# Eight small loads of the chunked S5 input issued one per hyena unit over eight units, where there were two per unit over four

## The reference

```python
h_c = modulate(ctx, norm_mix, cshift_mix, cscale_mix)
u_c = h_c @ w_in[:, :1024]                     # S5 input of the context
h_x = modulate(x, norm_mix, shift_mix, scale_mix)
u_x, hy_x, gates_x = split(h_x @ w_in)         # S5 input, hyena (3 x 1024), merge gates (2 x 2048)
y_x = readout(states(u_x, forward, seeded by the context's last state)) \
    + readout(states(u_x, backward, seeded by the context's first state))
x = x + gate_mix * mixer_output(u_x, y_x, hy_x, gates_x)   # GLU, long convolution, merge, w_out
x = x + gate_ffn * swiglu(modulate(x, norm_ffn, shift_ffn, scale_ffn), w_ffn_in, w_ffn_out)
return rms_norm(x, norm_f)
```

## Time and profile before

| | us |
|---|---|
| median of 3 runs | 2881.26 |
| lowest and highest run | 2880.14, 2881.98 |
| span of the profiled execution | 2886.0 |

### The profile page before, as it was taken

The page is one execution under the profiler, slowest core; times in us unless marked ns, Lnnn a source line. Parts: engine busy times, 40 slices in busy tenths (PEclk is TensorE's granted clock), DMA queues, the critical chain, the costliest instruction groups (busy, mean ns, idle before and its releaser), DMA issues.

```text
span 2886.0 us, 40851 instructions
## 1 busy us (share of the span) xinstructions
PE 2822.8 (98%) x17044; PEld 2456.8 (85%) x17044; DVE 1939.7 (67%) x2657; ACT 970.0 (34%) x1376; POOL 272.1 (9%) x475
## 2 busy tenths in 40 slices
PE   7999999999999999999989999999999999999997
PEld 2688788888888888887879999999999997888886
DVE  6546666985543777887768888888888774343445
ACT  4332333224442532221154444444443442222221
POOL 0001331001223001111100000000000000000000
PEclk9999999999999999999999999999999999999998
DMA  9726974334445537886544444444443335434333
GB/s 403 294 92 150 189 182 141 119 121 134 133 129 173 200 132 255 291 287 249 205 157 150 143 147 141 148 139 149 140 143 111 121 129 193 137 99 136 96 100 109
DMA packets 139531, 473.73 MB, mean 164 GB/s; under 512 B 24417, under 2 KB 24673, under 8 KB 134610
## 3 DMA queue, kind: packets, MB, share of 16 engines
q1 hardware_dynamic: 84226, 302.96, 31.8%
q0 software_dynamic: 47248, 156.09, 16.8%
q10 hardware_dynamic: 7872, 12.06, 1.2%
HBM read 426.53 MB, written 44.43 MB: 163 GB/s over the span
## 4 chain that ended last, share of the span: by engine, by line
PE 90%; DMA 4%; DVE 3%; ACT 2%; issue 1%; POOL 0%; ACTq 0%; DVEq 0%; SPq 0%; POOLq 0%
PE ps L2048 11%; PE ps L2050 10%; PE ps L2049 10%; PE ps L2303 10%; PE ps L2304 10%; PE ps L2305 10%; PE ps L2333 5%; PE ps L2334 5%; PE ps L2335 5%; DMA hw_raw<-in_w_in 2%; PE ps L2065 2%; PE ps L2018 1%; PE ps L2127 1%; DMA hw_raw<-in_w_out 1%; PE ps L2066 1%; PE ps L1959 1%
## 5 line engine op out<-in xcount | busy, mean ns | idle before, releaser
L1124 DVE TENSOR_TENSOR hw_lo<-hw_raw,hw_hi 128x1024 fp32r<-128x1024 f32 (+1 forms) x348 | 382.7, 1101 | 629.7 <-ACT hw_hi L680 628.0
L680 ACT ACTIVATE hw_hi<-hw_raw 128x1024 fp32r<-128x1024 f32 (+1 forms) x348 | 333.7, 961 | 1049.1 <-DMA hw_raw<-in_w_in 469.0
L1050 ACT ACTIVATE wx_hi<-wx 128x1024 fp32r<-128x1024 f32 x287 | 303.5, 1058 | 445.9 <-PE ps L2305 431.6
L1771 DVE TENSOR_TENSOR wx_lo<-wx,wx_hi 128x1024 fp32r<-128x1024 f32 x287 | 350.4, 1222 | 58.8 <-ACT wx_hi L1050 58.7
L2303 PE MATMUL ps<-t_hi,wx_hi 128*128 128x256 f32 x1312 | 371.3, 283 | 0.0
L2304 PE MATMUL ps<-t_lo,wx_hi 128*128 128x256 f32 x1312 | 371.3, 283 | 0.0
L2305 PE MATMUL ps<-t_hi,wx_lo 128*128 128x256 f32 x1312 | 371.3, 283 | 0.0
L2048 PE MATMUL ps<-h_hi,hw_hi 128*128 128x512 f32 x896 | 354.4, 396 | 3.7 <-DVE st_b L1389 2.6
L2050 PE MATMUL ps<-h_hi,hw_lo 128*128 128x512 f32 x896 | 350.6, 391 | 0.0
L2049 PE MATMUL ps<-h_lo,hw_hi 128*128 128x512 f32 x896 | 350.4, 391 | 0.0
L2303 PE MATMUL ps<-h_hi,wx_hi 128*128 128x256 f32 x984 | 278.6, 283 | 0.0
(11 more groups left out here) (359 smaller groups left out, 5187.6 us busy)
## 6 DMA issues: line engine op xcount, KB each, us to landing
wx<-in_w_fi SPq DMA_DIRECT2D x164, 512.0 KB, 3.3
hw_raw<-in_w_in SPq DMA_DIRECT2D x128, 512.0 KB, 4.2
ada1m<-in_w_ar POOLq DMA_DIRECT2D x128, 512.0 KB, 4.8
ada_mix<-in_w_ac SPq DMA_DIRECT2D x16, 2048.0 KB, 12.7
hw_raw<-in_w_fo SPq DMA_DIRECT2D x64, 384.0 KB, 3.1
hw_raw<-in_w_fo SPq DMA_DIRECT2D x64, 320.0 KB, 2.9
hw_raw<-in_w_glu SPq DMA_DIRECT2D x32, 512.0 KB, 4.8
hw_raw<-in_w_out SPq DMA_DIRECT2D x32, 512.0 KB, 4.4
```

Source lines behind the costliest of these rows:

```text
L680: act.activation(hw_hi[slot(n)][:, 0:width(n)], hw_raw[slot(n)][:, 0:width(n)], ACT.Copy).then_inc(w_hi, 1)
L1124: tt(hw_lo[s][:, 0:w], hw_raw[s][:, 0:w], hw_hi[s][:, 0:w].bitcast(F32), SUB).then_inc(w_lo, 1)
L1771: tt(wx_lo[o % 12][:, :], wx[o % 12][:, :], wx_hi[o % 4][:, :].bitcast(F32), SUB).then_inc(w_lo, 1)
```

## The change

In POOL's loop over the hyena units the eight calls `u8_load(1, j)`, j = 0 to 7, were spread as two per unit over v = 1 to 4. They become one per unit over v = 1 to 8 (`CH` is 8).

```diff
@@ -558,9 +558,8 @@
                 if v + 1 < NS:
                     for d in range(2):
                         in_slot(v + 1, d)
-                if 1 <= v < 5:
-                    for j in range(2 * v - 2, 2 * v):
-                        u8_load(1, j)
+                if 1 <= v < 1 + CH:
+                    u8_load(1, v - 1)
 
             pool.wait_ge(mt_rd, 2 * NS)
             c_slot(0)
```

## The result

The kernel became **slower**: 2890.47 us, the median of 15 runs, beside 2883.71 us for the kernel before, the median of 15 runs on the same chip. The ratio is 1.0024 with an interval of 1.0015 to 1.0033, which is +6.9 us (4.3 to 9.5). The forecast was -5.9 us, and its range, up to 2880.4, did not hold the time. Of the 15.1 us between the forecast of 2875.4 and this median, 2.4 belong to the kernel before, whose median was 2881.26 when the forecast was made. The profiled execution took 2893.49 us, with a span of 2891.7, which is 5.7 over the span before.

A forecast was written before the change was run, and what follows sets the result against it. TensorE, busy for 98% of the span, was taken to bound the kernel. The terms -7.2 + 0 + 1.3 = -5.9 us took 2881.26 to a forecast of 2875.4 us, range 2873.4 to 2880.4.

The forecast's parts named there:

- Term one: TensorE's units four to six: waits for late convolutions and the clock's fall go away; -7.2 us, bounds -7.2 and 0.
- rival 3: Hyena units: bursts make slices late, so TensorE's waits stay, spread over more units; 0 to -3 us; chance 0.12.
- Term two: POOL's units five to eight: one more load each, 0.65 us of issue, hidden behind waits for VectorE; 0 us.
- Term three: Before TensorE's group nine: a wait for the last load, now issued later; +1.3 us, bounds 0 and 8.2.
- a load alone: Landing time of a single load, 4.6 us, the low end for the last load's estimated landing of 6.5.
- Rival 4: Before group nine: last load lands after 13.4, TensorE waits 8.2 us, clock falls; +3.8 us, 2885.1; chance 0.08.
- All terms carry over: Terms are differences inside one stage, so -5.9 us from the profiled execution applies to the median 2881.26, giving 2875.4.

The follow-up runs named there:

- all but the first a unit earlier: Changed kernel, but two loads at the end of unit one, then one per unit, the last at unit seven; ratio 0.9993.
- load ahead of the tables: Changed kernel, but each load is issued ahead of the next unit's input table transfers, not behind them; ratio 0.9984.
- last load on SP: Changed kernel, but the eighth load goes by SP's queue behind weight slice 37, with its own semaphore; ratio 1.0019.
- eight at once: Changed kernel, but all eight loads are issued at the end of unit one; ratio 1.0019.
- 128 partitions, pairs: Schedule of the kernel before, two loads per unit over units one to four, each load as four transfers of one group to 128 partitions; ratio 0.9983.
- 128 partitions, one per unit: Changed kernel's schedule, each load as four transfers to 128 partitions, group nine waiting for all of them; ratio 1.0003.
- only the last late: Changed kernel, but pairs of loads at units one to three, one at unit four, none at five to seven, one at unit eight; ratio 1.0020.
- 128 partitions, by group: Changed kernel's schedule with four transfers to 128 partitions per load, each TensorE group from nine on waiting only for its own four; ratio 0.9991.
- the kernel before, again: The kernel before, unchanged, traced twice more, one profiled execution each; 2886.24 and 2888.08 us.

## Why the prediction was wrong, step by step

**Term one held.** The waits for a convolution are gone, and all 7.2 us of the earlier trace rows with them; rival 3 is out. Its reasons held less well. The share was to be 0.86 and is 0.93: (0.93 - 0.69) x 12.7 = 3.1 us of all sixteen engines for each load (2.8 by the mean of three clean units, 0.71), where I had 2.2 from the pairs. Slices land after 4.1 to 9.7 us, median 6.8, where I had 7 to 8; that this is still soon enough shows in the clean stretches.

**Term two held as a number.** The 0.65 us of issue on POOL show nowhere. Its remark that whoever needs the table transfers does so a unit or more later was wrong: VectorE waited until 373.00 for one issued at 364.70, and that made the last load late.

**Term three is the step that failed**, by its size: +(6.5 + 1.0 - 6.2) = +1.3 was the forecast, and 7.9 of wait plus 2.2 of clock, 10.1 us, came. The mechanism and the place were right, and the wait lies inside its bounds (0 to 8.2); with the clock, which had no part in them, it does not. Of the three numbers in it, the landing was 11.4 and not 6.5 (4.9 of the error), and the margin after all delays was 3.6 and not 5.2 (1.6 of it): against the 6.2 the issue was 2.6 us later, not 1.0, and for a transfer of tables, not for a slice. The 4.6 of "a load alone" was the wrong neighbour. It is the load issued at 199.8 us, in the S5 units, where the DMA share is 0.45 until it has landed; the other seven of the first half, also one at a time, land after 5.8 to 7.3, and the eight in the loop of the kernel before after 7.6 to 13.4, median 10.4. I had placed the landing between a load alone and the first of a pair, and had argued that the slowest loads had a backlog behind them that the change would take away. The last load has one too: at one load per unit the share in the three units ahead of it is 0.96, 0.99 and 0.96. My own number said otherwise because I took the price of a load from stretches whose share was already 1.04, full. The clock followed from it; I had let it fall only for the longer wait, and at 7.8 us and at 3.0 it fell. Even the forecast's own wait of 1.3 us would have left it open: after 1.43 us it did not fall, after 1.53 it did (last section).

**Rival 4 is what happened**: it had 11.0 us against 7.2, and 2885.1 us, at a chance of 0.08. It deserved more, since it and the forecast differed in one number for which the nearest rows, two loads beside table transfers, had 7.6 to 13.4. Its +3.8 us is the stage's +3.2 to within a microsecond; the measured +6.9 (4.3 to 9.5) is more than it gives, which is the next point.

**"All terms carry over" is not settled.** The stage in the profiles and the measured difference of nine kernels, each against the kernel before (stage mean 196.8 of three):

| Kernel | stage, us | difference of stage | measured |
|---|---|---|---|
| changed kernel (mean of three) | 201.0 | +4.2 | +6.9 |
| all but the first a unit earlier | 191.5 | -5.3 | -2.0 |
| load ahead of the tables | 190.7 | -6.1 | -4.6 |
| last load on SP | 200.3 | +3.5 | +5.5 |
| eight at once | 198.1 | +1.3 | +5.5 |
| 128 partitions, pairs | 190.7 | -6.1 | -4.9 |
| 128 partitions, one per unit | 192.4 | -4.4 | +0.9 |
| only the last late | 200.5 | +3.7 | +5.8 |
| 128 partitions, by group | 190.7 | -6.1 | -2.6 |

Every measured value lies above the stage's, the eight experiments by 2.9 us in the mean. The simplest reading is that the kernel before loses about 6.1 - 2.9 = 3.2 us to its pairs in an average execution, and not 6.1; then the changed kernel should stand at 201.0 - 190.7 - 3.2 = +7.1, and it measures +6.9. The other reading, that the new kernels lose time outside the stage, is not in the traces: the span less the stage is 2688.1 to 2689.3 us for the kernel before, and 2681.9 to 2690.7, mean 2685.1, for the eleven other traces. But the first reading is argued, not shown. The two repeats of the kernel before took 2886.24 and 2888.08 us, 3.1 and 4.9 over the median of its runs beside them (2883.15), and outside the stage its three profiled executions are 3.7 us longer than the others' mean. They may be no fair sample of it, in the stage or out of it. What it says for the forecast is that even without a wait the gain is not 7.2: the four versions whose stage is within a microsecond of clean (191.5 or 190.7 us) measure -2.0, -4.6, -4.9 and -2.6 us.

## What to carry to other kernels

When a change moves a transfer later, the margin is the whole question, and both of its ends belong to the stage as it will be: take the landing from rows with the same neighbours in flight, at the share that the new schedule will have, and not from between a lone one and a pair. A stretch whose DMA share is 1 says only how much time the transfers could get, not how much they would take (2.2 us for a load there, 2.8 at a share of 0.93). And a queue entry that waits for nothing belongs ahead of those that wait for a compute engine: here that alone was worth 11.5 us between the changed kernel (+6.9) and the version with the load ahead (-4.6).

## What the hardware showed that I had not expected

A load of 192 KB that writes 16 partitions makes the packets of the weight slices longer (0.25 us for 0.20 in the mean of the stage, 0.28 in one unit), takes 7.5 to 11.4 us to land in the loop of the changed kernel, and as long on SP's queue. The same bytes in four transfers over 128 partitions leave them at 0.20 to 0.22. Each of the four lands after 4.8 to 6.6 us; from the first issue to the last landing it is 6.5 to 8.3. Both forms move pieces of 384 bytes, so that the size of the piece is not the difference. Whether it is the number of partitions or the cut into four transfers, and which part of the way is the narrow one, no run here tells.

The clock fell (the granted clock went from 1.00 to 0.5 for some us) after or during waits of TensorE, in this stage, of 1.53 us (only the last late), 2.27 and 3.21 us (the kernel before, again), 2.63 us (the kernel before), 2.96 us (only the last late), 5.86 us (eight at once), 6.84 us (last on SP) and 7.44 to 7.76 us (the changed kernel, three times). Each fall cost 1.6 to 3.3 us (what the units are longer than 12.71, less the wait). After 0.44 us (all but the first a unit earlier), 1.06 (the kernel before, again) and 1.43 (128 partitions, one per unit) it did not fall. TensorE: Matmul & The Clock Gate, Part 1, in the Trainium skill says that an idle stretch brings the lower clock; the five waits of 5.86 us and more agree. For the short ones the length alone does not decide: at the wait of the earlier trace rows in the FFN there was no fall after 2.68 us, nor after 2.54 (changed kernel), 2.52 (load ahead) and 2.46 us (eight at once), but there was one after 2.25 (only the last late) and after 2.56 us (128 partitions, one per unit). And outside the stage it fell at 796.9 us of the kernel before, after a wait of 1.43 us. What decides it at the short ones, no run here tells.
